# A second quarter of one expert load placed outside the weight ring, and the router's scratch and the down biases moved to other buffers

## What is computed

```python
h = rms_norm(x, norm_ffn_g)
logits = h @ w_router + b_router
top_val, top_idx = lax.top_k(logits, 4)          # 4 of 32 experts for each token
gates = jax.nn.softmax(top_val, axis=-1)
...
g = xb @ w_gate[e] + b_gate[e]                   # for the tokens xb of expert e
u = xb @ w_up[e] + b_up[e]
g = jnp.minimum(g, 7.0); u = jnp.clip(u, -7.0, 7.0)
y = ((u + 1.0) * g * jax.nn.sigmoid(1.702 * g)) @ w_down[e] + b_down[e]
out = out.at[tokens].add(y * gate)
```

## Time and profile before

| | us |
|---|---|
| median of 3 runs | 1103.12 |
| lowest, highest | 1102.29, 1103.67 |
| the profiled execution, whole | 1103.43 |
| the profiled execution, span of the trace | 1101.6 |

### The profile page before, as it was taken

One profiled execution on the slowest core, in us unless ns is written; L12 is line 12 of the kernel. 1 busy time (PEld: TensorE's weight loads), 2 busy tenths in 40 slices (PEclk: granted clock), 3 DMA queues, 4 the chain that ended last, 5 costly groups with the idle time before them and its releaser, 6 DMA issues.

```text
span 1101.6 us, 12895 instructions
## 1 busy us (share of the span) xinstructions
PE 1048.0 (95%) x5462; PEld 503.8 (46%) x5462; DVE 302.9 (27%) x622; ACT 131.0 (12%) x243; POOL 13.1 (1%) x18
## 2 busy tenths in 40 slices
PE   9999999999999999999999988989898989998996
PEld 8999996534433443344342422433243324332432
DVE  5977888420302121121111111211102020201122
ACT  2212350310000001001000100001000100000012
POOL 1200000000000000000000000000000000000000
PEclk9999999999999999999999999999999999999998
DMA  8974377999999999999999999999999999999996
GB/s 327 427 295 162 134 290 304 349 425 428 435 430 430 434 430 432 433 432 430 434 432 430 434 433 427 434 434 430 431 434 430 432 434 430 432 433 432 424 427 257
DMA packets 26799, 438.17 MB, mean 398 GB/s; under 512 B 5008, under 2 KB 6416, under 8 KB 9616
## 3 DMA queue, kind: packets, MB, share of 16 engines
q1 hardware_dynamic: 26192, 435.05, 93.3%
q10 hardware_dynamic: 576, 2.69, 0.6%
HBM read 436.28 MB, written 1.05 MB: 397 GB/s over the span
## 4 chain that ended last, share of the span: by engine, by line
PE 62%; DMA 35%; DVE 1%; SPq 1%; ACT 1%; issue 1%; another core or an unknown queue 0%; DVEq 0%; POOL 0%; POOLq 0%
DMA ring<-in_experts 35%; PE ps L2075 24%; PE ps L2124 12%; PE ps L1634 8%; PE ps L1985 3%; PE ps L2133 3%; PE ps L1813 2%; PE ps L1629 2%; PE ps L1878 2%; PE ps L1683 1%; PE ps L2113 1%; PE ps L1994 1%; SPq L509 1%; ACT region_va L857 0%
## 5 line engine op out<-in xcount | busy, mean ns | idle before, releaser
L2075 PE MATMUL ps<-ring,xT 128*64 128x512 f32 x2044 | 461.9, 607 | 24.3 <-DMA ring<-in_experts 24.3
L2075 PEld LDWEIGHTS ps<-ring,xT 128*64 128x64 f32 x2044 | 145.0, 139 | 313.7 <-issue 284.2
L2124 PE MATMUL ps<-ring,region_va 128*64 128x512 f32 x1024 | 227.9, 595 | 20.1 <-ACT region_va L857 11.5
L2124 PEld LDWEIGHTS ps<-ring,region_va 128*64 128x64 f32 x1024 | 73.2, 137 | 153.1 <-issue 126.7
L1529 DVE TENSOR_SCALAR g<-ps 128x1024 f32<-128x1024 f32 x16 | 19.6, 1225 | 348.4 <-PE ps L2075 342.5
L1634 PE MATMUL ps<-ring 128*128 128x128 f32 x784 | 89.7, 276 | 0.1
L1634 PEld LDWEIGHTS ps<-ring 128*128 128x128 f32 x784 | 88.5, 192 | 0.9 <-DVE ring L943 0.3
L1475 DVE TENSOR_TENSOR xT<-ps,g_ffn 128x512 f32<-128x512 f32 x30 | 20.8, 692 | 189.1 <-PE ps L1985 189.1
L1551 DVE TENSOR_SCALAR region_va<-ps 128x512 f32<-128x512 f32 x32 | 22.1, 692 | 182.8 <-PE ps L2075 182.8
L1985 PEld LDWEIGHTS ps<-sel,x 128*128 128x128 f32 x480 | 55.4, 192 | 9.5 <-issue 9.5
L2133 PE MATMUL ps<-g,g_T 128*128 128x512 f32 x128 | 59.2, 605 | 0.0
(11 more groups left out here) (271 smaller groups left out, 536.8 us busy)
## 6 DMA issues: line engine op xcount, KB each, us to landing
ring<-in_experts SPq DMA_DIRECT2D x77, 4096.0 KB, 46.3
ring<-in_experts SPq DMA_DIRECT2D x28, 2048.0 KB, 12.7
ring<-in_head SPq DMA_DIRECT2D x13, 2048.0 KB, 17.2
ring<-in_experts SPq DMA_DIRECT2D x13, 1024.0 KB, 8.8
ring<-in_first SPq DMA_DIRECT2D x7, 384.0 KB, 6.4
ring<-in_experts SPq DMA_DIRECT2D x5, 512.0 KB, 9.1
ring<-in_experts ACTq DMA_DIRECT2D x2, 1024.0 KB, 9.7
ring<-in_experts SPq DMA_DIRECT2D x1, 1536.0 KB, 6.0
```

The costliest lines, as they stand in the source:

```text
L2075: last = mm(bank(banks + half)[rows, :], xT[:, 2 * m + c, rows], weights[:, k], start=False, stop=m == 3 and c == 1, skip_group_check=True)
L2124: last = mm(bank(first + half)[rows, :], hTm[:, 2 * m + c, rows], w[:, c, half, k], start=m == 0 and c == 0, stop=m == 3 and c == 1, skip_ ...
```

## The change

1. `ASIDE_FROM` goes from the fourth quarter to the third: both upper quarters, (1,0) and (1,1), of the first pair's fourth gate load are loaded outside of the ring, (1,1) into `g_r` as before and (1,0) into `r_va`. Both places in the ring are filled early with the second pair's. The 512 KB load of the second pair's quarter (1,0), issued in `load_iteration` before, is gone (`SECOND_PAIR_LOADS` counts one fewer).
2. `r_va` has to be empty for that. The router's small results go to `gx`, `gs` and `small`, with the same shapes and the same instructions.
3. The down biases come in three pieces of 256, 128 and 128 columns into `g_T` (router weights until then), `logit_parts` and `ranks` (the two small matrices of the rank products, now one buffer). The last is in use until `rk_done`, so SP waits for that, a wait that it didn't have.
4. `start_y` works on the three pieces: 12 products where it had 4, with the same columns in sum.
5. PE's wait for what is set aside stands a quarter load later, ahead of (1,0), and is for both quarters.

```diff
-ASIDE_LOAD, ASIDE_FROM = 3, 3 * D
+ASIDE_LOAD, ASIDE_FROM = 3, 2 * D
-SECOND_PAIR_LOADS = [5, 4, 3, 2, 2, 2]
+SECOND_PAIR_LOADS = [5, 3, 3, 2, 2, 2]
...
-        su_b = sb("su_b", P, BF16)
-        one_b = sb("one_b", P, BF16)
+        ranks = sb("ranks", P)
+        su_b, one_b = (ranks[:, k * P // 2:(k + 1) * P // 2].bitcast(BF16) for k in range(2))
...
+        bd4 = [(0, 2 * P, gT_r[:, :]), (2 * P, 3 * P, logit_parts), (3 * P, 4 * P, ranks[:, :])]
-        bd4 = r_va[:, 0:W512]
-        aside = g_r[:, :]
-        aside_w = aside.rearrange("p (k n) -> p k n", k=2)
+        aside_w = [r[:, :].rearrange("p (k n) -> p k n", k=2) for r in (r_va, g_r)]
...
-                                load_columns(row, p, SLOT_COLS // 2, ASIDE_FROM if p == ASIDE_LOAD else SLOT_COLS,
-                                             unit_loaded[m])
+                                if p != ASIDE_LOAD:
+                                    load_columns(row, p, SLOT_COLS // 2, SLOT_COLS, unit_loaded[m])
...
             sp_.wait_ge(rt_done, 2)
-            sp_.dma_start(aside, experts_v[ASIDE_LOAD // 2][:, SLOT_COLS + ASIDE_FROM:2 * SLOT_COLS]
-                          ).then_inc(aside_loaded, 16)
+            at = SLOT_COLS + ASIDE_FROM
+            sp_.dma_start(g_r[:, :], experts_v[ASIDE_LOAD // 2][:, at + D:at + 2 * D]).then_inc(aside_loaded, 16)
             sp_.wait_ge(ssq2_ready, 4)
-            sp_.dma_start(bd4, b_down4).then_inc(ld_bd4, 16)
+            sp_.dma_start(r_va[:, :], experts_v[ASIDE_LOAD // 2][:, at:at + D]).then_inc(aside_loaded, 16)
+            sp_.wait_ge(rk_done, 1)
+            for lo, hi, part in bd4:
+                sp_.dma_start(part, b_down4[:, lo:hi]).then_inc(ld_bd4, 16)
...
-                pe.wait_ge(ld_bd4, 16)
+                pe.wait_ge(ld_bd4, 48)
                 for r in range(4):
                     rows = slice(r * E, (r + 1) * E)
-                    last = mm(bank(Y_B + r), gates_T[rows, :], bd4[rows, :], start=True, stop=True)
+                    for lo, hi, part in bd4:
+                        last = mm(bank(Y_B + r)[:, lo:hi], gates_T[rows, :], part[rows, :], start=lo == 0, stop=True,
+                                  skip_group_check=True)
...
-                    if first_pair and m == ASIDE_LOAD:
-                        pe.wait_ge(aside_loaded, 16)
...
+                            if first_pair and which == 0 and (m, c, half) == (ASIDE_LOAD, 1, 0):
+                                pe.wait_ge(aside_loaded, 32)
```

More of the change, by code:

```diff
@@ L328, in build @@
         nr_i = sb("nr_i", 1, I32)
-        gx = sb("gx", NT * E)[:, :].rearrange("p (a n) -> p a n", a=NT)
+        gx_r = sb("gx", NT * (E + 4))
+        gx = gx_r[:, 0:NT * E].rearrange("p (a n) -> p a n", a=NT)
         rkx = sb("rkx", NT * NEXT)[:, :].rearrange("p (a n) -> p a n", a=NT)
@@ L341, in build @@
         gates_T = gs_r[:, P:2 * P]
-        bd4 = r_va[:, 0:W512]
-        aside = g_r[:, :]
-        aside_w = aside.rearrange("p (k n) -> p k n", k=2)
[L346 to L351, removed]
+        aside_w = [r[:, :].rearrange("p (k n) -> p k n", k=2) for r in (r_va, g_r)]
+        lg = gx_r[:, :].rearrange("p (a e) -> p a e", a=NT)
+        left = gs_r[:, P:P + NT * (E + 4)].rearrange("p (a e) -> p a e", a=NT)
+        ex = left[:, :, 0:E]
+        mask = gs_r[:, 0:NT * E].rearrange("p (a e) -> p a e", a=NT)
+        rt, top8 = small[:, 16:32], small[:, 32:48].rearrange("p (a e) -> p a e", a=NT)
+        mask_b = small[:, 48:80].bitcast(BF16).rearrange("p (a e) -> p a e", a=NT)
         weight = rt[:, 13:15]
@@ L2073, in gate_or_up @@
                                 rows = slice(k * SLOTS, (k + 1) * SLOTS)
-                                weights = aside_w if first_pair and 4 * which + m == ASIDE_LOAD and c == half == 1 else w[:, c, half]
+                                weights = aside_w[half] if first_pair and 4 * which + m == ASIDE_LOAD and c == 1 else w[:, c, half]
                                 last = mm(bank(banks + half)[rows, :], xT[:, 2 * m + c, rows],
```

## The result

| | before | after |
|---|---|---|
| median, us | 1103.16 (8 runs) | 1105.84 (8 runs) |
| lowest, highest | 1102.29, 1103.67 | 1104.82, 1107.89 |
| the profiled execution, span | 1101.6 | 1104.2 |

The ratio is 1.0025, 95% interval [1.0016, 1.0034]: 2.7 us slower where 1.1 us faster was forecast, and 2.1 us above the upper end of the range.

The account below looks back on a forecast made before the run. The transfer stream at 431 GB/s, counted from its last dry stretch at the router's end, was taken as the bound. Terms: -1.22 + 0.1 = -1.1 us, giving 1102.3 us profiled, 1102.0 median; range 1100.8 to 1103.7.

Parts of the forecast that it names:

- (a): Router's end: the quarter load requested earlier fills holes in the transfer stream; gain 1.22 us.
- (b): Down biases in three pieces: more short rows add 0.15 us of stream work, which the holes still take.
- (c): SP's new wait for rk_done before the last bias piece: cost 0, with 1.6 us to spare.
- (d): PE's wait for what is set aside, near 222.0 us: cost 0, 7 us to spare.
- (f): Router's scratch on other buffers, same instructions and shapes: cost 0.
- (e): start_y: PE 1.8 us later, delaying the second pair's loads from 227.40 us; queued transfers cover it, cost 0.1 us.
- Rival 3: Row groups in start_y: a hole of 1 us or so near 229 us; 1103.0 us, chance 0.08.
- Rival 1: Router's end: the holes don't fill; gain 0.7 us, 1102.4, or 1103.4 if all stay; chance 0.13.
- Rival 2: Fixed transfer time paid in turn for two more transfers before the second pair's loads; 1106.2 us, chance 0.04.
- rival 4: PE sets the end, so the moved quarter brings nothing and start_y costs 1.8 us; 1104.9 us, chance 0.03.

Follow-up runs that it names:

- e1: The changed kernel with start_y's products reordered so that the four row groups take turns for each piece; 1103.3 us, ratio 1.0002.
- e7: The changed kernel with start_y cut to 128 of 512 columns, row groups taking turns; 1101.69 us, ratio 0.9986.
- e6: The kernel before with start_y cut to 128 of its 512 columns; 1102.88 us.
- e11: e9 with start_y also moved behind the first up load's products; 1102.14 us, ratio 0.9991.
- e12: The kernel before with start_y behind the first up load, second pair's first eight slots in halves, third pair's first 4 MB as two requests; 1103.32 us.
- e3: The kernel before with the down biases requested as three transfers into the same buffer, products unchanged; 1103.15 us, ratio 1.0002.
- e2: The kernel before with only start_y altered to the changed kernel's three-piece order, row group by row group; 1105.39 us, ratio 1.0027.
- e13: e2 with the third pair's first 4 MB request made as two of 2 MB; 1105.11 us, ratio 1.0016.
- e4: e1 with start_y moved behind the first up load's products; 1102.94 us, ratio 1.0004.
- e14: The kernel before with 4, 7 or 14 unread 128-column products (the padding) added behind start_y; 1104.65, 1105.87 and 1107.78 us.
- e8: e1 with the second pair's first eight slots, instead of five, requested in halves; 1103.0 us, ratio 0.9996.
- e9: e8 with the third pair's first 4 MB request made as two of 2 MB; 1102.85 us, ratio 0.9999.

## Why the prediction was wrong

**The bound** was read rightly for most of the program: from 290 us on the stream runs at 431 GB/s whatever was changed, and the time follows the last ring load. The sentence that a microsecond on PE in the middle costs nothing is the one that failed. From 290 us on it holds: with 14 products added SP's request near 293 us is still 3.2 us late, and the rate from there on is 431 GB/s as before. From 225 to 290 us PE has no wait on transfers, and yet the transfers wait on PE, as the waits of SP show in the kernel before (205 to 290 us; in total, times, longest):

```profile
SPq L509 <- PE ps L2075: 45.5, 13, 10.9
```

A full ring says that PE has a lead, not that the transfer queue has one. The profile before shows that queue in the times to landing.

**(a)** The bytes were right and the holes did take them in part (0.8 us ahead at 225 us). The forecast stopped there. Requests behind that point come when PE frees slots, so bytes that pass earlier are taken out of the queue at 227 us. In e1 all of it was given back within 15 us, so in the changed kernel the term of -1.22 us is worth nothing. It is 1.2 us only in e7 against e6 and in e11 against e12.

**(b)** 0.15 us was foreseen; e3's median is 0.17 us above that of its group, in an interval from -0.9 to +1.2 us, so the size is not measured, only that it is small. The pieces landed by 212.6 us (206.46 + 6.1), foreseen by 214.

**(c), (d)** as foreseen, and nothing speaks against (f), which no run took by itself: SP issued the three pieces at 205.60, 205.97 and 206.46 and the next load at 208.49, unhindered; PE did not wait for what is set aside (the products with `region_va` follow those of the ring at once, at 221.88).

**(e)** is the step that failed. Its first half was right: 1.8 us later was foreseen, 1.7 came. The second half took 3.3 us of queue as spare, made of a landing time less 2.1 us for a small transfer, and let the late PE and the moved request use it up to the last 0.3 us. Those 0.3 us mean 4.8 us to landing, and 5.4 were measured, so the queue's length came out nearly as worked out; wrong was that the rate holds until it has shrunk to that. The kernel before had no depth to spare for a late PE: 1.0 us of padding cost 1.6 us. And the lateness was counted once, while it is met again at 265 to 290 us in the profiles of the changed kernel, e2 and the padding of 7 and 14 (with 4 it is not: 426 and 436 GB/s). The term was 0.1 us and is 2.4 us by e1 and e2, 2.8 by the padding of 7.

**The rivals.** Rival 3 named the mechanism and the place, "near 229 us", but at 1 us and a chance of 0.08. Rival 1 was half right: the filled stretches stay at 347 to 363 GB/s. Rival 2, at 1106.2 the nearest of all to the measured time, falls by e3 and e1: the nearness is luck. So is that of rival 4, at 1104.9, which falls by the chain, that still ends with a ring load, and by PE's waits for ring loads after 600 us, which grew from 33 to 39 us. No rival said that the gain could be given back behind the place where it is made.

**What stays open.** Whether and why a microsecond of lateness costs more than itself (1.5 to 1.7 by the medians). That the stream restarts slowly after it ran short, at more than one place, agrees with the stretches of e2 and e13, but no run took the restart by itself. Nor was a whole kernel tried in which the down biases take less of PE's time at this place, which by e7 would be worth something to the changed kernel.

## What to carry to other kernels

Where a prefetch ring hands over from filling to steady state, as at 225 us here, moving bytes earlier may only borrow from the queue behind; look at the next stretch in which requests depend on the consumer, and at the time to landing there, before booking the gain. In that stretch the consumer's own work can count in full, here 1.5 to 1.7 us for one by the medians, although it waits for nothing. And products on separate row groups of PE should alternate between the groups: grouping them by three made 1.1 us into 2.7 here.

## What the runs showed of the hardware

In these profiles the stream lost rate while a queue still stood. The first 1 MB request after the gap behind `start_y` takes 2.4 us for its bytes, and this is its time to landing beside the rate from 225 to 240 us, each from one profiled execution:

| | to landing, us | GB/s |
|---|---|---|
| e12, e6, e4, e3, before | 9.0, 8.5, 8.2, 8.0, 7.9 | 422, 429, 424, 418, 428 |
| e11 | 7.4 | 421 |
| e7 | 7.2 | 428 |
| e14 with 4, e1, e13, e8 | 7.2, 7.0, 6.9, 6.8 | 391, 397, 376, 403 |
| e9, e2, e14 with 7 | 6.3, 6.3, 6.2 | 401, 392, 395 |
| after, e14 with 14 | 5.4, 4.7 | 360, 358 |

For the kernel after, its row in the view of issues (KB each, us to landing):

```profile
ring<-in_experts SPq DMA_DIRECT2D x1, 1024.0 KB, 5.4
```

So the rate is 418 to 429 GB/s where the request takes 7.4 us or more, and 358 to 403 where it takes 7.0 or less, still 4.6 us beyond its bytes and not only the 2.1 us that a small transfer takes. At 7.2 us both are seen, 428 in e7 and 391 in e14 with 4, and between 6.2 and 7.0 us the rate doesn't follow the time, so this is a border seen at one place of one program and not a law. The engines' busy share stays at 0.93 to 1.03 through it: the same bytes keep the engines busy for longer (0.97 at 360 GB/s, 1.03 at 428). A share near 1 is no sign of a full queue.
